# A two-layer mixer block on one core: attention's preparation moved into the delta rule's block, output projection split by column parts

## The chip, the core and the metric

The kernel runs on one core of a Trainium2 chip. The core has TensorE (PE in the profile, with PEld for its weight loads), VectorE (DVE), ScalarE (ACT), GpSimd (POOL) and SyncE (SP), which here mostly issues DMAs. The metric is the device time of one execution in microseconds. Lower is better.

## What is computed

Two layers run one after the other. Each takes 1152 tokens (1024 latent ones, which are tiles 0 to 7 of 128, and 128 context ones, tile 8, called CTX) of width 1024. Cut to what matters here:

```python
h = rmsnorm(x, norm_pre) * (1 + scale) + shift
z = h @ w_in                                   # u_pool, g_pool, q, k, v, g_attn, qkv_d, b, a, g_delta
o_pool  = pool_mixer(u_pool)
o_attn  = attention(q, k, v)                   # 8 query heads, 2 key heads, head size 64, softmax
o_f, s_f = gated_delta_chunked(..., forward)   # chunks of 64, state S (64 x 64) per head, 4 heads
o_b, s_b = gated_delta_chunked(..., backward)
o_delta = rmsnorm(o_f + flip(o_b))
y = (silu(gates) * concat(o_pool, o_attn, o_delta)) @ w_out
x = x + gate * rmsnorm(y, norm_post)
```

Latent queries see 1024 latent keys and 128 cached ones. Context queries see only the 128 context keys.

## The kernel before, in words

`build` loops over the layers with `Fori` and calls four stages: `enter` (modulation, input projection), `delta_rule`, `attention` and `project_out`. Each stage has a block of its own: every engine gets a program, engines wait for one another by semaphores only, and a stage begins when all engines have ended the one before. `clear` then resets the semaphores.

Every 32-bit operand of a precise product is split in two fp32r parts, high and low, and the product is made of high·high, high·low and low·high.

**`delta_rule`.** Nine turns, one for each token tile, prepare for both scan directions (d = 0, 1) small matrices that are stored in the tile's place. `delta_order` gives the order by hand. The recurrence comes after the last turn: for s = 0 to 16, `scan(s, d)` (L1056) is four 64x64 matmuls that multiply the state, and VectorE (L1177) adds the additive part and writes the next state. TensorE waits with `s_done` for that before the next step of the same direction. `output(t)` (L1070, 32 small matmuls) forms the outputs of tile t into banks 2 to 7, three pairs of PSUM banks in turn, and VectorE adds them to `of` (L1183). `OUTPUTS` lists which tile follows which step: most follow steps 11 to 17. ScalarE and GpSimd have no part in the recurrence.

**`attention`.** It begins with preparation. VectorE splits the keys of each two tiles in a high and a low part (L1636, L1640), TensorE transposes four blocks (L1548), ScalarE copies them to KH (L1443) and VectorE copies the high rows on to KO (L1645). GpSimd splits the queries (L1368, L1370), TensorE transposes the high parts (L1469, item "hi"), ScalarE copies them (L1414). Then come the maxima: for each query block TensorE multiplies the high parts (L1490, L1495) and VectorE reduces 1152 scores of each row to a maximum (L1576, L1579), which is written beside the low part of the queries. The low parts are transposed after it (item "lo", L1477). `first` is the list of these steps for the pairs 0 and 1, `call_bank` gives the first ten maxima banks 0 and 4 in turn. `scores(0)` (L1530, L1531) waits for the ten maxima and for KO. The main loop then runs over 73 steps (`ATTN_STEPS`): scores of a key tile, exponentials on ScalarE (L1438), sums on GpSimd (L1384), weighted values on TensorE (L1540). In its slots, fixed beforehand, stand the preparation of later pairs, reciprocals, gates and the delta rule's output norm. GpSimd squares `of` for that norm (L1390) early in the block.

**`project_out`.** Eight blocks of 128 channels make up the branches (`branch(k)`), and `w_out` comes in eight DMAs of 512 KB (L1693). For each k ScalarE makes the high part of the branch (all 1152 tokens, L1709) and then of the weights (L1711), VectorE makes the low parts (L1743, L1745). TensorE does tile 0 while they come (L1766, six matmuls for each k, waits `low` and `w_split`), then 32 matmuls (L1773) that spread the column of the gate over all partitions, from diagonals that GpSimd made (L1728). Tiles 1 to 8 follow. For each tile: Square with a sum on ScalarE (L1721), root on GpSimd (L1732, L1734), scaling on VectorE (L1750), adding x on GpSimd (L1737), and a DMA.

## Time and profile before

| | us |
|---|---|
| median of 3 runs | 1920.18 (1915.82 to 1921.32) |
| profiled execution, time | 1911.73 |
| its span | 1910.0 |
| PE busy in the span | 1698.0 (89%) |
| DVE, ACT, POOL busy | 1003.2, 608.2, 983.5 |
| mean granted TensorE clock | 0.945 |

The two layers are alike and lie 957 us apart. Layer 1 has its recurrence from 537 to 555, attention's block from 555 to 830, the output projection from 830 to 957. Busy shares are means over stages with different limits; a matmul is counted until its modelled end, so a busy TensorE is not one at its peak. The granted clock is 1.00 (2.4 GHz) or 0.50 (1.2 GHz), or a mean of them where a stretch has both.

### The profile page before, as it was taken

The page shows a single profiled execution, that of the slowest core. Times are in us where ns is not written, and L with a number is a line of the kernel's source. Part 1 is how long each engine was busy: PE and PEld are TensorE (multiplying, and loading weights), DVE is VectorE, ACT ScalarE, POOL GpSimd, SP SyncE. Part 2 cuts the span into 40 slices and gives each one's busy share as a digit, 9 for nine tenths or more (in the row PEclk, how much of TensorE's full clock was granted, in tenths as well). Part 3 has the DMA queues.
Part 4 walks back from the last instruction along what each step waited for, and adds up shares of the span by engine and source line. Part 5 has one row for each costly group of instructions (what it writes and reads, how often), then busy time and mean ns, then how long its engine had stood idle before and what let it go on. Part 6 is the DMA issues. An engine that isn't in the chain of part 4 may idle for free. (4 is left out here: it accounts for less than half of the span.)

```text
span 1910.0 us, 40869 instructions
## 1 busy us (share of the span) xinstructions
PE 1698.0 (89%) x17404; PEld 1375.7 (72%) x17404; DVE 1003.2 (53%) x1488; ACT 608.2 (32%) x1180; POOL 983.5 (51%) x894
## 2 busy tenths in 40 slices
PE   4999999799968899959849999997999688999597
PEld 3898999789955455538728989997899554554386
DVE  2746237277755785551126462272777657855511
ACT  4322211244412445441033122112444134444400
POOL 1003593199823878872310034930998238788632
PEclk8999999999986999989969999999999879999899
DMA  9301113100000020022283011131000000100222
GB/s 338 114 24 51 43 56 111 58 21 15 4 22 1 6 61 12 11 110 89 77 307 133 19 54 52 56 111 59 20 15 4 22 1 11 56 12 11 111 88 88
DMA packets 70959, 117.22 MB, mean 61 GB/s; under 512 B 10097, under 2 KB 42097, under 8 KB 70769
## 3 DMA queue, kind: packets, MB, share of 16 engines
q1 hardware_dynamic: 69840, 114.18, 17.5%
q8 instruction: 140, 2.29, 0.5%
q10 hardware_dynamic: 928, 0.34, 0.1%
q14 instruction: 51, 0.41, 0.1%
HBM read 95.03 MB, written 19.47 MB: 60 GB/s over the span
## 5 line engine op out<-in xcount | busy, mean ns | idle before, releaser
L1384 POOL TENSOR_TENSOR attn_accp<-attn_accp,attn_pr 128x1024 f32<-128x1024 f32 x112 | 269.1, 2403 | 50.8 <-ACT attn_pr L1438 44.4
L93 PE MATMUL ps<-h_hi,in_w_hi 128*128 128x384 f32 (+1 forms) x816 | 276.0, 338 | 5.0 <-DVE h_lo L456 4.9
L94 PE MATMUL ps<-h_lo,in_w_hi 128*128 128x384 f32 (+1 forms) x816 | 274.7, 337 | 0.0
L95 PE MATMUL ps<-h_hi,in_w_lo 128*128 128x384 f32 (+1 forms) x816 | 274.5, 336 | 0.0
L1579 DVE TENSOR_REDUCE attn_ql<-ps 128x1 f32<-128x1152 f32 x128 | 172.8, 1356 | 127.8 <-PE ps L1495 127.7
L1438 ACT ACTIVATE attn_pr<-ps 128x512 f32<-128x512 f32 x292 | 159.0, 595 | 193.0 <-PE ps L1531 191.1
L93 PEld LDWEIGHTS ps<-h_hi,in_w_hi 128*128 128x128 f32 (+1 forms) x816 | 150.1, 184 | 13.2 <-issue 6.7
L94 PEld LDWEIGHTS ps<-h_lo,in_w_hi 128*128 128x128 f32 (+1 forms) x816 | 150.2, 184 | 3.9
L95 PEld LDWEIGHTS ps<-h_hi,in_w_lo 128*128 128x128 f32 (+1 forms) x816 | 150.2, 184 | 3.9
L1530 PEld LDWEIGHTS ps<-attn_QH,attn_KH 128*128 128x128 f32 x292 | 55.9, 191 | 126.0 <-issue 54.9
L1540 PE MATMUL ps<-attn_pr,z 128*64 128x512 f32 x520 | 142.2, 626 | 0.0
L890 POOL TENSOR_TENSOR delta_ML<-delta_EK,local 128x256 f32<-128x256 f32 x180 | 131.0, 749 | 16.1 <-PE ps L926 15.2
L1530 PE MATMUL ps<-attn_QH,attn_KH 128*128 128x512 f32 x292 | 133.0, 456 | 0.3 <-ACT attn_pr L1438 0.3
L926 PE MATMUL ps<-delta_TR,delta_ML 64*64 64x64 f32 x2880 | 112.5, 224 | 17.8 <-POOL delta_ML L890 11.3
L288 POOL TENSOR_TENSOR in_scratch<-zz 128x1175 f32<-128x1175 f32 x4 | 10.6, 2639 | 228.1 <-ACT zz L716 228.1
L93 PE MATMUL ps<-in_w_hi,h_hi 128*128 128x256 f32 x432 | 124.6, 288 | 0.0
L1766 PE MATMUL ps<-out_w_hi,out_b_hi 128*128 128x512 f32 x288 | 92.9, 404 | 34.8 <-DVE out_w_lo L1745 34.8
L94 PE MATMUL ps<-in_w_lo,h_hi 128*128 128x256 f32 x432 | 122.9, 284 | 0.0
L95 PE MATMUL ps<-in_w_hi,h_lo 128*128 128x256 f32 x432 | 122.8, 284 | 0.0
L1531 PE MATMUL ps<-attn_QL,attn_KO 65*128 65x512 f32 x292 | 117.6, 403 | 0.0
L926 PEld LDWEIGHTS ps<-delta_TR,delta_ML 64*64 64x64 f32 x2880 | 98.2, 137 | 26.6 <-DVE delta_TR L1154 12.2
L1495 PE MATMUL ps<-attn_KH,attn_QH 128*128 128x384 f32 x384 | 97.9, 369 | 12.9 <-DVE attn_ql L1579 12.5
(239 smaller groups left out, 3617.2 us busy)
## 6 DMA issues: line engine op xcount, KB each, us to landing
in_w<-in_w_in SPq DMA_DIRECT2D x22, 1024.0 KB, 6.0
zz<-in_w_mod SPq DMA_DIRECT2D x8, 2048.0 KB, 13.6
gates<-in_gate SPq DMA_DIRECT2D x48, 192.0 KB, 1.9
attn_gt<-gates SPq DMA_DIRECT2D x34, 256.0 KB, 2.6
z<-in_w_mod SPq DMA_DIRECT2D x4, 2048.0 KB, 10.2
out_w<-in_w_out SPq DMA_DIRECT2D x16, 512.0 KB, 6.2
out_y<-out_y SPq DMA_DIRECT2D x10, 512.0 KB, 2.9
delta_GB<-gc_rows SPq DMA_DIRECT2D x36, 128.0 KB, 2.9
```

What stands on the lines that cost most here:

```text
L93: nc.tensor.matmul(out, a_hi(i), b_hi(i), start=(i == 0), stop=False)
L94: nc.tensor.matmul(out, a_hi(i), b_lo(i), start=False, stop=False)
L95: last = nc.tensor.matmul(out, a_lo(i), b_hi(i), start=False, stop=(i == n - 1))
L890: nc.gpsimd.tensor_tensor(pairs(ML[d][:, i % 2]), EA[d][:, j % 3, :, 0], level_mask(i, d), ALU.mult).then_inc(ml_done, 1)
L926: last = nc.tensor.matmul(heads(bank, off)[rows(c), h, :], lhs(rows(c), h), rhs(rows(c), h), start=True, stop=True)
L1384: nc.gpsimd.tensor_tensor(acc, a, pr[:, n % 4], ALU.add).then_inc(pool_added, 1)
L1438: nc.scalar.activation(pr[:, n % 4, e], ps[:, e, :], ACT.Exp, scale=HD ** -0.5).then_inc(p_done, 1)
L1495: last = nc.tensor.matmul(ps[:, bank + c, 0:GRP], QH[:, p % 3, blk // 2, col:col + P], KH[:, g, GRP * c:GRP * c + GRP], start=True, stop=True)
L1530: nc.tensor.matmul(ps[:, e, :], KH[:, g, ks], QH[:, p % 3, e, :], start=True, stop=False)
L1531: nc.tensor.matmul(ps[:, e, :], KO[0:HD + 1, g, ks], QL[0:HD + 1, p % 2, e, :], start=False, stop=True).then_inc(st_done, 1)
L1540: nc.tensor.matmul(ps[HD * e:HD * e + HD, 2 + p % 2, :], values(p, kt, e), pr[:, n % 4, e], start=(kt == 0), stop=(kt == STEPS_OF[p] - 1)) ...
L1579: nc.vector.tensor_reduce(ql[:, a % 4, blk, HD:HD + 1], ps[:, bank:bank + 3, 0:GRP], AX_XY, ALU.max).then_inc(mx_read, 1)
```

## The change

1. `delta_rule` and `attention` become one block, `delta_and_attention`. Attention's tensors are laid over memory of the delta rule: those of the preparation over tensors of the nine turns, which are free after the last turn (`au_out`), the others over `gq1` and the states, free after the last output (`o_out`).
2. Key turns (L1548) and the first four query turns (L1469) are done inside the recurrence: keys after steps 2, 3, 4, 5, 6, queries after steps 8, 10, 12, 14. They use banks 7 and 6, so outputs have two bank pairs instead of three.
3. The high parts of keys and of the first four query blocks move to ScalarE, the keys' low parts to GpSimd, the copies to KO to ScalarE. GpSimd's ones row of KO, squares and the split of block 4 come after.
4. In `first`, the low parts' turns stand between the last maxima. The turn of query block 4 comes after `scores(0)`.
5. `project_out`: the branch's high and low parts in two column parts, tokens 0 to 383 ahead of the weights, the rest behind them (waited for before tile 3). The gate's spreading comes first on TensorE, as a product of the broadcast column and the identity; GpSimd's diagonals are gone.
6. The last tile is done in two column halves, with sums of each half added on GpSimd, and x added on VectorE.

```diff
+        place_in = scan_memory
+        gq1 = sb("gq1", [P, NT, 6, P])
+        S = both("S", [P, S_CTX + 1, 2, HD])
+        place_in = turn_memory
...
+        turn_memory.close()
+        scan_memory.close()
+        attn = attention(nc, io, m, l, ctx, au_out, o_out, state_out_done)
...
+                attn["cache"](sp)
                 for d in range(2):
                     sp.wait_ge(s_done[d], 2)
...
                 sp.wait_ge(state_out_done, 32)
+                attn["sync"](sp)
...
-                    b = 2 + 2 * (n_out % 3)
-                    if n_out >= 3:
-                        pe.wait_ge(o_out, n_out - 2)
+                    b = 2 + 2 * (n_out % 2)
+                    if n_out >= 2:
+                        pe.wait_ge(o_out, n_out - 1)
...
+                    attn["turns"](pe, s)
                     for t in OUTPUTS.get(s, []):
                         output(t)
+                attn["tensor"](pe)
...
-    first += [("max", 1, 0, b) for b in range(4)] + [("lo", 0, 0), ("lo", 0, 1)] + [("max", 1, 1, b) for b in range(4)]
-    first += [("lo", 1, 0), ("lo", 1, 1), ("hi", 2, 0)]
+    first += [("max", 1, 0, b) for b in range(4)] + [("max", 1, 1, 0), ("lo", 0, 0), ("max", 1, 1, 1), ("lo", 0, 1), ("max", 1, 1, 2),
+                                                     ("lo", 1, 0), ("max", 1, 1, 3), ("lo", 1, 1), ("hi", 2, 0)]
...
+        def key_low(j):
+            pool.wait_ge(k_high, j + 1)
+            for ks, k in keys_of(j):
+                last = nc.gpsimd.tensor_tensor(khl[:, ks, :, HD:P], k, khl[:, ks, :, 0:HD], ALU.subtract)
+            last.then_inc(k_split, 1)
+
+        pool.wait_ge(au_out, STEPS)
+        for j in range(4):
+            key_low(j)
+        split(0, 0)
+        split(0, 1)
+        key_low(4)
+        split(1, 0)
+        split(1, 1)
+        pool.drain()
+        nc.gpsimd.memset(KO[HD:HD + 1].bitcast(F32), -1.0).then_inc(ones_done, 1)
+        pool.drain()
+        pool.wait_ge(o_out, NT)
+        pool.wait_ge(state_out_done, 32)
+        nc.gpsimd.tensor_tensor(osq[:], of[:], of[:], ALU.mult).then_inc(o_sq, 1)
+        split(2, 0)
...
+        for j in range(4):
+            key_high(j)
+        query_high(0, 0)
+        keys_turned(0)
+        keys_turned(1)
+        query_high(0, 1)
+        keys_turned(2)
+        keys_turned(3)
+        key_high(4)
+        query_high(1, 0)
+        keys_turned(4)
+        evict(("hi", 0, 0))
+        query_high(1, 1)
+        evict(("hi", 0, 1))
+        for j in range(3):
+            keys_copied(j)
+        evict(("hi", 1, 0))
+        for j in range(3, 5):
+            keys_copied(j)
...
+    def key_turn(pe, j):
+        pe.wait_ge(k_split, j + 1)
+        if j >= 2:
+            pe.wait_ge(k_act, j - 1)
...
+    def turns(pe, s):
+        if s in KEY_TURNS:
+            key_turn(pe, KEY_TURNS.index(s))
+        if s in QUERY_TURNS:
+            query_turn(pe, *ASKS[QUERY_TURNS.index(s)])
...
+        for item in first[4:-1]:
+            work(item)
+        pe.wait_ge(cache_in, 32)
+        scores(0)
+        work(first[-1])
...
-K_BANKS = (7, 0, 1, 2, 3)
+K_BANKS = (7, 6, 7, 6, 7)
+KEY_TURNS = (2, 3, 4, 5, 6)
+QUERY_TURNS = (8, 10, 12, 14)
...
                 for k in range(KD):
-                    nc.scalar.activation(b_hi[:, k, :], branch(k), ACT.Copy).then_inc(high, 1)
+                    nc.scalar.activation(b_hi[:, k, COLS[0]], branch(k)[:, COLS[0]], ACT.Copy).then_inc(high, 1)
+                for k in range(KD):
                     act.wait_ge(w_in[k], 16)
                     nc.scalar.activation(w_hi[:, k], wst[:, k], ACT.Copy).then_inc(w_high, 1)
...
+                for k in range(KD):
+                    nc.scalar.activation(b_hi[:, k, COLS[1]], branch(k)[:, COLS[1]], ACT.Copy).then_inc(high, 1)
...
-                for c in range(2):
-                    for k in range(KD):
-                        last = nc.gpsimd.tensor_scalar(diag[:, c, P * k:P * k + P], m["ident"], m["gcol"][:, k, c:c + 1], None, ALU.mult)
-                    last.then_inc(diag_done, 1)
...
+                        for i in range(2):
+                            part = slice(512 * i, 512 * i + 512)
+                            nc.vector.scalar_tensor_tensor(out=y[t % 2][:, part], in0=ps[:, 2 * (t % 2) + i, :], scalar=rs[:, t:t + 1],
+                                                           in1=grow[:, c, part], op0=ALU.mult, op1=ALU.mult)
+                            dve.drain()
+                            nc.vector.tensor_tensor(y[t % 2][:, part], y[t % 2][:, part], x[:, t % 2, part], ALU.add).then_inc(added, 1)
...
+                for c in range(2):
+                    for k in range(KD):
+                        last = nc.tensor.matmul(ps[:, 4 + 2 * c + k // 4, P * (k % 4):P * (k % 4) + P],
+                                                m["gcol"][:, k, c:c + 1].broadcast_to([P, P]), m["ident"], start=True, stop=True)
+                    last.then_inc(spread, 1)
                 for t in range(NT):
                     if t >= 2:
                         pe.wait_ge(scaled, t - 1)
+                    if t == 3:
+                        pe.wait_ge(low, 2 * KD)
```

## Rows read from the trace of the kernel before

**Rows 1.** Windows: stretch, its length, busy time of each engine, granted clock, DMA share.
```profile
537.00:555.00 18.00, 15.21 (x560) 13.41 (x560) 11.94 (x43) 0.00 (x1) 0.00 (x0) 1.00 0.05 11
...
568.00:595.00 27.00, 21.41 (x73) 16.81 (x74) 14.32 (x16) 5.45 (x10) 3.96 (x8) 0.50 0.00 1
...
831.00:860.00 29.00, 17.80 (x79) 13.31 (x80) 20.26 (x16) 17.07 (x18) 24.45 (x16) 0.82 0.47 181
860.00:949.00 89.00, 88.86 (x387) 72.10 (x386) 10.28 (x8) 10.02 (x19) 25.21 (x24) 1.00 0.26 89
...
1512.00:1550.00 38.00, 22.59 (x85) 17.13 (x86) 26.11 (x27) 7.75 (x13) 15.68 (x20) 0.60 0.07 22
```
**Rows 2.** Timeline, recurrence of layer 1: start us, us, engine, line, operation, idle before.
```profile
540.65 0.45 PE L1056 MATMUL ps<-delta_S,zz 64*64 64x64 f32 x8 [0.16 <-DVE delta_S L1177]
...
541.49 0.45 PE L1056 MATMUL ps<-delta_S,zz 64*64 64x64 f32 x8 [0.16 <-DVE delta_S L1177]
...
553.68 1.36 DVE L1183 TENSOR_TENSOR of<-ps,of 128x256 f32<-128x256 f32 x3 [0.98 <-PE ps L1070]
```
**Rows 3.** Timeline, begin of attention's block, layer 1.
```profile
559.15 0.73 POOL L1370 TENSOR_TENSOR attn_ql<-z,attn_qhh 128x256 f32<-128x256 f32 x1
...
560.63 0.46 DVE L1640 TENSOR_TENSOR attn_khl<-z,attn_khl 128x256 f32<-128x256 f32 x1
...
561.65 4.07 POOL L1390 TENSOR_TENSOR attn_osq<-of 128x2304 f32<-128x2304 f32 x1
561.92 4.09 DVE L1640 TENSOR_TENSOR attn_khl<-z,attn_khl 128x256 f32<-128x256 f32 x1
```
**Rows 4.** Source view of one line: duration ns min/median/max, first and last start.
```profile
L1154 DVE TENSOR_TENSOR delta_TR<-delta_TR,ps x180: 380/410/423, 384.0 to 1483.7; 128x256 f32<-128x256 f32 x180
```
**Rows 5.** Timeline, first maxima, low parts' turns and first scores, layer 1.
```profile
578.57 2.62 DVE L1579 TENSOR_REDUCE attn_ql<-ps 128x1 f32<-128x1152 f32 x2 [0.70 <-PE ps L1495]
...
584.94 2.27 PE L1495 MATMUL ps<-attn_KH,attn_QH 128*128 128x384 f32 x6
...
590.22 1.05 PE L1477 MATMUL ps<-masks,attn_ql 128*65 128x128 f32 x4
...
594.53 0.78 PE L1530 MATMUL ps<-attn_QH,attn_KH 128*128 128x512 f32 x1
```
**Rows 6.** Timeline, the same in layer 2, from the last output.
```profile
1510.64 1.36 DVE L1183 TENSOR_TENSOR of<-ps,of 128x256 f32<-128x256 f32 x3 [0.99 <-PE ps L1070]
...
1546.07 0.76 PE L1495 MATMUL ps<-attn_KH,attn_QH 128*128 128x384 f32 x3 [0.50 <-DVE attn_ql L1579]
...
1546.66 0.60 PE L1477 MATMUL ps<-masks,attn_ql 128*65 128x128 f32 x4
...
1550.32 0.48 PE L1530 MATMUL ps<-attn_QH,attn_KH 128*128 128x512 f32 x1
```
**Rows 7.** Timeline, the last sums of attention's loop, layers 1 and 2.
```profile
823.41 1.08 PE L1507 MATMUL ps<-attn_accp,ones 128*64 128x512 f32 x4 [3.63 <-POOL attn_accp L1384]
...
1775.33 1.08 PE L1507 MATMUL ps<-attn_accp,ones 128*64 128x512 f32 x4 [3.62 <-POOL attn_accp L1384]
```
**Rows 8.** Timeline, output projection of layer 1: first matmul, spreading, tile 1.
```profile
837.64 1.19 PE L1766 MATMUL ps<-out_w_hi,out_b_hi 128*128 128x512 f32 x2 [13.15 <-DVE out_w_lo L1745]
...
856.59 3.73 PE L1773 MATMUL ps<-z,ones 128*128 128x128 f32 x32
...
860.08 0.71 PE L1766 MATMUL ps<-out_w_hi,out_b_hi 128*128 128x512 f32 x2
```
**Rows 9.** Windows, while the weights of the output projection arrive (last column GB/s).
```profile
839.00:841.00 2.00, 2.00 (x6) 1.46 (x5) 2.00 (x2) 2.00 (x3) 2.00 (x2) 0.50 1.01 410
```
**Rows 10.** Timeline, the end of layer 2.
```profile
1900.40 1.02 ACT L1721 ACTIVATE out_y<-ps 128x1024 f32<-128x1024 f32 x1 [9.95 <-PE ps L1766]
...
1902.53 1.28 DVE L1750 SCALAR_TENSOR_TENSOR out_y<-ps,out_rs,z 128x1024 f32<-128x1024 f32 x1 [9.78 <-POOL out_rs L1734]
1903.89 2.34 POOL L1737 TENSOR_TENSOR out_y<-out_y,out_x 128x1024 f32<-128x1024 f32 x1 [1.40 <-DVE out_y L1750]
```

More of the change, by code:

```diff
@@ L1122, in _ @@
                 delta_order(phase)
+                attn["scalar"](act)
             @block.vector
@@ L1758, in _, with products @@
                         pe.wait_ge(scaled, t - 1)
+                    if t == 3:
+                        pe.wait_ge(low, 2 * KD)
                     tk = slice(P * t, P * t + P)
+                    def products(k, halves):
+                        for a, b in ((b_hi, w_hi), (b_hi, w_lo), (b_lo, w_hi)):
+                            for i in halves:
+                                last = nc.tensor.matmul(ps[:, 2 * (t % 2) + i, :], a[:, k, tk], b[:, k, 512 * i:512 * i + 512],
+                                                        start=(k == 0 and a is b_hi and b is w_hi), stop=(k == KD - 1 and a is b_lo))
+                        return last
+                    if t == NT - 1:
+                        for i in range(2):
+                            for k in range(KD):
+                                last = products(k, (i,))
+                            last.then_inc(product, 1)
+                        continue
                     for k in range(KD):
```

821 lines of the change are left out of this document (412 added, 409 removed).

## The prediction, made before the changed kernel was run

> **What bounds the kernel now.** I read the windows first, to see which stretches of a layer are not bound by steady work, then the timeline inside them. Attention's loop and tiles 1 to 8 of the output projection are steady: in the latter TensorE is busy 88.86 of 89 us at the full clock, 11.1 us a tile [rows 1], and no edit removes a matmul there. What is open is three stretches of each layer.
>
> First, from the last output of the recurrence (553.68 + 1.36 = 555.0 [rows 2]) to the first scores at 594.5 [rows 5] there are 39.5 us in which no scores are made; in layer 2 it is 1512.0 to 1550.3, 38.3 us [rows 6]. No engine is the bound: from 568 to 595 TensorE is busy 21.4 of 27 us but at 1.2 GHz, VectorE 14.3 and ScalarE 5.5 [rows 1]. It is a chain through four engines. Meanwhile in the recurrence (537 to 555) ScalarE and GpSimd do nothing and TensorE is busy 15.2 of 18 us [rows 1]; that is a chain too, 0.84 us a step from one L1056 row to the next [rows 2], with only 0.16 us of TensorE idle in front of each step.
>
> Second, the first tile of the output projection with the spreading behind it: 837.64 to 860.08, 22.4 us for 11.1 us of matmuls and 3.7 us of spreading [rows 8]. VectorE sets the pace: its low parts of branch and weights fill 20.3 of the 29 us [rows 1].
>
> Third, the end of each layer, a chain of ScalarE 1.02, GpSimd, VectorE 1.28, GpSimd 2.34 us and a DMA [rows 10].
>
> **The preparation that moves into the recurrence.** Nine turns of four transposes are added to TensorE's queue between steps. Four of them take 0.60 us at 2.4 GHz with the drain of the last (low parts' turn [rows 6]), so about 0.54 us of issue. A step is 0.84 us, of which the two directions fill 0.46 in one piece (0.45 of a row is one direction with its drain, and the other is issued within it), so a step with a turn is at least 0.46 + 0.54 = 1.0 us: 0.2 us more with the semaphore. Steps 12 and 14 also have outputs and no gap left, so there the turn costs its whole 0.54. Seven times 0.2 and two times 0.54 is 2.5 us.
>
> To this come waits, since the queue is in order and the recurrence's next steps stand behind each turn. A key turn needs ScalarE's high part (0.4 us for each two tiles, by the 0.46 us of VectorE's subtraction of that size [rows 3] as the nearest), GpSimd's low part (0.73 [rows 3]), and for the third turn on the copy of two turns before. GpSimd's first four low parts follow one another from about 538.3 to 541, ahead of turns at 539.3, 540.3, 541.3 and 542.3: no wait. The fifth stands on GpSimd behind two query splits, and on ScalarE behind four copies and two query halves; I make it ready at 545.4, and TensorE asks at 543.7: 1.7 us of wait. The query turns find their operands ready. The outputs with two bank pairs in place of three wait once, 0.3 us. Sum: the recurrence becomes **4.5 us longer** in each layer (bounds 2.5, all waits hidden, and 10, a wait like the fifth's at half of the nine turns).
>
> On VectorE nothing is added, but GpSimd now works beside its state additions. In the turns L1154, of the same kind (one input from PSUM, one from SBUF), takes 380 to 423 ns beside a GpSimd that never rests [rows 4]; so I add nothing. The contrast: a subtraction with both inputs in SBUF took 4.09 us beside GpSimd's squares of 4.07 us, where the same one took 0.46 alone [rows 3]. The Trainium skill ("SBUF — State Buffer", section "Who interferes with whom") says that a VectorE instruction with two SBUF inputs contends with a GpSimd one that reads SBUF and that one with a single SBUF input does not; the rows agree, and by it the loss of rows 3 goes away with the move, as my sum has it anyway.
>
> SP's queue: the four loads of the cache and the norm column go out ahead of the stores of the state, a few issues later for these, and only work after the recurrence waits for them. The gate loads wait for `o_out`, with tens of microseconds before their first reader. GpSimd's squares (4.07) run beside maxima, whose inputs are in PSUM alone.
>
> **From the last output to the first scores**, new: `o_out` and the first product 0.8, two small maxima 1.4, eight maxima of 1.31 (2.62 for two [rows 5]) 10.5, the last low turn 0.6 and hops 0.7: 14.0 us. This is if VectorE is the bound. A product of three matmuls takes 0.76 and a turn 0.60 at 2.4 GHz [rows 6], 1.36 as rows, nearer 1.2 in issue; they just fit beside 1.31. At 1.2 GHz a product is 2.27 / 2 = 1.14 and a turn 1.05 [rows 5]; the three maxima with a turn ahead of them would take 2.2 each and the others 1.42, together 17.8 us. The removed waits of ScalarE and the block's change are in the difference. I add 2 us a layer for the clock being at its lower level part of the time.
>
> Layer 1: 39.5 - 14.0 - 2 - 4.5 = **19.0**. Layer 2: 38.3 - 14.0 - 2 - 4.5 = **17.8**. In layer 1 the loop also begins at 1.2 GHz: from first scores to the last sums 228.9 us (594.53 to 823.41), against 225.0 in layer 2 (1550.32 to 1775.33), where the clock had risen before [rows 5 to 7]. With the clock up in both, layer 1 gains **3.9**.
>
> **The output projection's first tile.** The first matmul waits for the first weights' low part (837.64), a DMA and two splits later; that stays. After it a k costs TensorE 11.1 / 8 = 1.38 us; the weights come at 410 GB/s [rows 9], 0.52 MB in 1.28 us; VectorE needs for the weights' part 20.3 / 16 = 1.27 us as now; ScalarE 17.07 / 16 = 1.07 [rows 1]. TensorE is then the bound: tile 0 ends at 837.6 + 11.1 = 848.7 and tile 1 follows at once, 11.3 us earlier than 860.08. The spreading fills time before 837.6 in which TensorE was idle for 13.15 us [rows 8]: 3.7 us, or 7.5 at 1.2 GHz. The second column parts are 2/3 of the first form's work, some 7 us on each of ScalarE and VectorE, ended by 853; tile 3, which waits for them, starts at 871, and tile 2, which needs the first tile's scaling, at 860. GpSimd's diagonals have no reader on the path now. Gain **11.3** in each layer; bounds 5.7 (the spreading and 2 us) and 12.
>
> **The last tile.** Square over half a bank pair saves 0.5, an extra addition on GpSimd costs 0.35, VectorE's two scalings and two additions of 512 columns take 2.7 with drains against 1.28 + 2.34 + 0.1: 1.0, the last DMA is half as large: 0.3. **1.5** in each layer, bounds 0 and 2.5.
>
> **Sum:** 19.0 + 17.8 + 3.9 + 2 x 11.3 + 2 x 1.5 = 66.3 us. The profiled execution took 1911.7, so 1845.4. It lies 8.5 us under the median of 1920.2; I take the gain from the median: **1854 us**. (That the two differ by 0.4% is a reason for a wide range.) A measurement of this kernel can tell about 0.3% from no change.
>
> **Rivals.**
> A. *The clock stays low.* After the recurrence TensorE works in pieces again: 0.76 us in each 1.31 us of the first five large maxima. In layer 2 it granted 2.4 GHz in such a stretch (L1495 at 0.76 [rows 6]); in layer 1 it was at 1.2 GHz from 568 to 595 with 79% busy [rows 1]. If it falls and stays low into the loop, preparation costs 3.8 in place of 2 a layer, and both loops are like layer 1's: 3.6 + 7.8 = 11.4 us more, 1865. [...] Against: it need only be held, since the recurrence ends at the full clock (1.00 from 537 to 555 [rows 1]) and the maxima now follow at once. The Trainium skill ("TensorE: Matmul & The Clock Gate", section "A second HAM failure mode: psum-queue depth-cycling") says that small idle pieces between groups of matmuls, when PSUM banks are cycled, let the clock swing between its two levels; by it this rival would happen in part, with the time just worked out as its end.
>
> B. *The first tile stays fed slowly*, by the arrival of weights or by ScalarE, and only the spreading and 2 us are gained: 11.2 us more, 1865.
>
> C. *The recurrence waits more*, up to the 10 us bound: 11 us more, 1865.
>
> D. *Everything hides and the clock is held*: no 1.7 us wait and no 2 us: 7 us less, 1847.
>
> E. *Slower.* One mechanism: the turns stand in TensorE's queue ahead of the recurrence's steps, and each waits for a chain through ScalarE, GpSimd, TensorE and ScalarE. If none of it overlaps the steps, a key turn costs 0.4 + 0.73 + 0.6 + 0.6 and four hops, 2.7 us, a query turn 3.0 (two high parts), 25.5 us a layer, and TensorE so thinned out falls to 1.2 GHz, where its 15.2 us of the recurrence would add up to 12. Against my 4.5 that is 33 us a layer more, all of the gain; with rival A's loops, 1854 + 66 + 8 = 1928, slower. It decides from 3.7 us of wait at each of nine turns. Against it: ScalarE and GpSimd have nothing else to do then, and their parts of 0.4 and 0.73 us are shorter than the 0.84 us step.
>
> **How the numbers follow.** Forecast 1854: 0.50. A 0.18, B 0.12, C 0.06, D 0.09, E 0.02; that the gain is cut by something not seen here, 0.03. The range that holds 8 in 10 goes from D to A and B with a second one of them in part, and takes in half of the 8.5 us between profile and median: 1841 to 1873. Faster by over 0.3%: 0.96, within 0.3%: 0.02, slower: 0.02.
>
> **What would show it.** Recurrence: 18 us before from its begin to the last output (537 to 555), about 22.5 after, with one wait for GpSimd's keys at step 6. First scores 14 to 18 us after the last output. Maxima back to back on VectorE. First matmul of the projection still 7 us into its block, tile 1 11.1 us later. Last tile: two VectorE additions, no GpSimd one. Wrong would be: waits at several turns, low clock in loops, weights waited for by ScalarE beyond the first.

## The result, and the profile after

The changed kernel takes 1854.19 us (median of four executions, 1847.7 to 1859.95), the kernel before 1918.0 (1913.52 to 1921.32) beside it: a ratio of 0.967, 95% interval 0.964 to 0.969. The profiled execution took 1847.7 us with a span of 1846.0, where that of before had 1910.0. The forecast was 1854, its range 1841 to 1873.

Read in the same order as before, the windows first (stretch, length, busy time of PE, PEld, DVE, ACT and POOL, granted clock, DMA share, GB/s). They are of the changed kernel, layer 1: recurrence, last output to first scores, begin of attention's loop, and of the output projection tiles 1 to 8 and (last line) tile 0.

```profile
536.20:559.60 23.40, 20.40 (x596) 17.41 (x596) 11.95 (x43) 11.92 (x28) 8.70 (x11) 1.00 0.08 20
559.60:575.00 15.40, 12.12 (x47) 9.70 (x48) 11.90 (x11) 1.79 (x3) 6.97 (x7) 0.67 0.11 36
575.00:586.00 11.00, 8.12 (x32) 4.75 (x30) 2.71 (x2) 3.99 (x8) 0.00 (x0) 0.84 0.00 1
...
827.30:916.00 88.70, 88.70 (x385) 71.94 (x383) 15.23 (x14) 13.88 (x25) 25.21 (x24) 1.00 0.26 89
816.10:827.30 11.20, 11.16 (x49) 9.11 (x50) 10.69 (x10) 9.80 (x12) 0.00 (x0) 1.00 0.76 309
```

ScalarE and GpSimd, which had nothing to do in the recurrence [rows 1], now work 11.9 and 8.7 us there. The timeline of that stretch, changed kernel, TensorE's turns and VectorE's state additions:

```profile
542.16 0.66 PE L1550 MATMUL ps<-masks,attn_khl 128*128 128x128 f32 x4
...
543.24 0.29 DVE L1190 TENSOR_TENSOR delta_S<-ps,zz 128x128 f32<-128x128 f32 x1 [0.67 <-PE ps L1066]
...
544.84 0.66 PE L1550 MATMUL ps<-masks,attn_khl 128*128 128x128 f32 x4 [1.42 <-POOL attn_khl L1412]
...
545.92 0.29 DVE L1190 TENSOR_TENSOR delta_S<-ps,zz 128x128 f32<-128x128 f32 x1 [2.16 <-PE ps L1066]
...
559.20 0.42 DVE L1196 TENSOR_TENSOR of<-ps,of 128x256 f32<-128x256 f32 x1 [0.99 <-PE ps L1080]
```

One turn of nine waits: the fifth key turn waits 1.42 us for GpSimd's low part, and the state addition behind it comes 2.68 us after the last one. From the first state addition (536.67) to the end of the last output (559.62) it is 22.95 us where it was 17.5 [rows 2], and 22.7 in layer 2. Then the maxima and the first scores, layer 1, and the first scores of layer 2:

```profile
565.59 2.62 DVE L1660 TENSOR_REDUCE attn_ql<-ps 128x1 f32<-128x1152 f32 x2 [0.22 <-PE ps L1587]
570.25 1.36 DVE L1660 TENSOR_REDUCE attn_ql<-ps 128x1 f32<-128x1152 f32 x1 [0.39 <-PE ps L1587]
...
574.66 0.62 PE L1569 MATMUL ps<-masks,attn_ql 128*65 128x128 f32 x4 [1.69 <-DVE attn_ql L1660]
575.04 0.48 PE L1623 MATMUL ps<-attn_QH,attn_KH 128*128 128x512 f32 x1
...
1496.38 0.48 PE L1623 MATMUL ps<-attn_QH,attn_KH 128*128 128x512 f32 x1
```

The first scores follow the last output by 15.4 us in layer 1 and 15.5 in layer 2 (last output's end 1480.91) where it was 39.5 and 38.3 [rows 5, 6]. The window above has the clock at 0.67: it fell to 1.2 GHz at about 561 and came back at about 571, and fell once more for some 3 us near 582. The end of the loop and the first matmul of the projection:

```profile
801.46 1.98 PE L1599 MATMUL ps<-attn_accp,ones 128*64 128x512 f32 x4 [3.36 <-POOL attn_accp L1407]
...
816.14 0.70 PE L1868 MATMUL ps<-out_w_hi,out_b_hi 128*128 128x512 f32 x2 [0.56 <-DVE out_w_lo L1831]
```

From 816.1 on TensorE is busy 11.16 of 11.2 us, then 88.70 of 88.70: tile 1 follows tile 0 at once, where 22.4 us lay between their begins [rows 8]. And the last tile of layer 2, in halves:

```profile
1838.61 0.19 POOL L1810 TENSOR_TENSOR out_ss<-out_half 128x1 f32<-128x1 f32 x1 [5.96 <-ACT out_y L1799]
...
1839.88 0.75 DVE L1842 SCALAR_TENSOR_TENSOR out_y<-ps,out_rs,z 128x512 f32<-128x512 f32 x1 [9.72 <-POOL out_rs L1814]
1840.71 0.69 DVE L1845 TENSOR_TENSOR out_y<-out_y,out_x 128x512 f32<-128x512 f32 x1
...
1842.15 0.69 DVE L1845 TENSOR_TENSOR out_y<-out_y,out_x 128x512 f32<-128x512 f32 x1
```

TensorE's last product ends at 1837.81, the span at 1846.04: 8.23 us, where it was 9.67 before, 1.4 less.

### The profile page after: what moved, and what is told of

It reads as the page before. It is cut to its first block and busy times, and to the rows that moved or that the text cites. A ratio compares the mean times of both kernels' runs of the same rounds, so it can differ in the third digit from the quotient of the medians.

```text
span 1846.0 us, 40839 instructions
## 1 busy us (share of the span) xinstructions
PE 1678.0 (91%) x17404; PEld 1366.1 (74%) x17404; DVE 978.3 (53%) x1476; ACT 624.1 (34%) x1238; POOL 929.1 (50%) x858
## 5 line engine op out<-in xcount | busy, mean ns | idle before, releaser
L936 PE MATMUL ps<-delta_TR,delta_ML 64*64 64x64 f32 x2880 | 112.2, 223 | 17.3 <-POOL delta_ML L899 11.3
L1587 PE MATMUL ps<-attn_KH,attn_QH 128*128 128x384 f32 x384 | 97.3, 366 | 12.9 <-DVE attn_ql L1660 11.9
L352 DVE CAST in_w_hi<-in_w 128x2048 fp32r<-128x2048 f32 (+1 forms) x24 | 28.2, 1176 | 152.3 <-DMA in_w<-in_w_in 152.3
## 6 DMA issues: line engine op xcount, KB each, us to landing
zz<-in_w_mod SPq DMA_DIRECT2D x8, 2048.0 KB, 13.6
z<-out_y SPq DMA_DIRECT2D x9, 512.0 KB, 10.5
```

Of the source, the lines that this page charges most:

```text
L936: last = nc.tensor.matmul(heads(bank, off)[rows(c), h, :], lhs(rows(c), h), rhs(rows(c), h), start=True, stop=True)
L1587: last = nc.tensor.matmul(ps[:, bank + c, 0:GRP], QH[:, p % 3, blk // 2, col:col + P], KH[:, g, GRP * c:GRP * c + GRP], start=True, stop=True)
```

## The experiments

All runs in one table, since one reading goes through them: the time from the first state addition to the end of the last output ("rec") and from there to the first scores ("prep"), both layers, and the loop from first scores to the last sums. "The projection" in the text is the time from its first product to the end of its last one: 111.2 us before, 99.9 and 99.8 in the changed kernel. "Ratio" is to the kernel before on the same chip, with its 95% interval; runs without one are single executions.

| kernel | us | ratio | rec + prep, L1 | rec + prep, L2 | loop L1, L2 |
|---|---|---|---|---|---|
| before | 1918.0 | 1 | 17.5 + 39.5 | 17.4 + 38.3 | 228.9, 225.0 |
| changed | 1854.2 | 0.967 (0.964-0.969) | 23.0 + 15.4 | 22.7 + 15.5 | 226.4, 226.4 |
| e10 changed again | 1855.2 | 0.968 (0.965-0.970) | 23.8 + 14.2 | 24.8 + 14.3 | 226.4, 227.6 |
| e1 attention alone | 1881.5 | 0.980 (0.975-0.984) | 24.8 + 14.2 | 24.7 + 14.2 | 226.4, 226.4 |
| e2 projection alone | 1895.2 | 0.989 (0.985-0.993) | 17.9 + 39.5 | 18.6 + 38.6 | 228.5, 225.1 |
| e3 no column parts | 1866.5 | 0.974 (0.971-0.977) | 25.2 + 14.2 | 23.2 + 15.3 | 226.3, 226.4 |
| e4 turns behind | 1873.2 | 0.977 (0.974-0.980) | 19.3 + 28.2 | 19.2 + 27.3 | 224.6, 232.1 |
| e5 fifth key earlier | 1853.7 | | 22.7 + 15.3 | 23.0 + 15.1 | 226.4, 226.4 |
| e6 fillers | 1855.4 | 0.965 (0.960-0.970) | 24.6 + 13.7 | 24.9 + 13.6 | 228.3, 226.8 |
| e7 old order | 1864.7 | | 24.6 + 16.8 | 25.3 + 16.8 | 228.7, 228.8 |
| e8 fillers, fifth key | 1850.8 | 0.963 (0.959-0.968) | 22.7 + 13.4 | 23.3 + 13.3 | 227.0, 225.5 |
| e9 more fillers | 1853.2 | 0.967 (0.965-0.969) | 21.3 + 13.6 | 21.2 + 13.4 | 226.8, 227.8 |
| e11 fewer fillers | 1840.3 | 0.960 (0.958-0.961) | 20.8 + 13.3 | 21.0 + 13.3 | 227.0, 225.4 |
| e12 last turn only | 1846.5 | 0.962 (0.960-0.963) | 21.2 + 15.6 | 21.4 + 13.3 | 228.7, 234.2 |

**e1, attention alone.** `project_out` is that of the kernel before.

```diff
+        diag = flat[:, 3 * D:5 * D].rearrange("p (c d) -> p c d", d=D)
...
-        COLS = [slice(0, GRP), slice(GRP, T)]
...
```

> The changed kernel with the output projection of the kernel before. Theory (my sum, each part on its own): the parts add up. The attention part is worth, by the profiles of before and after, 18.6 + 2.4 us in layer 1 and 17.5 - 1.4 us in layer 2, with 0.9 us for an earlier begin of the recurrence: about 38 us under the kernel before (ratio 0.980), the projection's stretches as in before: 29 us from the block's begin to tile 1. Rival (the parts share a gain, most of all through TensorE's clock, whose mean over the span rose from 0.945 to 0.963): the attention part alone gives under 30 or over 46 us, and tile 0 of the projection does not take its old 22.4 us.

Measured 0.980 of before, 39 us (0.0205 x 1917; 31 to 47 by the interval), as the theory had it. The projection took 111.2 us in both layers, as before.

**e2, projection alone.** The kernel before with the new `project_out`.

```diff
-        diag = flat[:, 3 * D:5 * D].rearrange("p (c d) -> p c d", d=D)
...
+        COLS = [slice(0, GRP), slice(GRP, T)]
...
```

> The kernel before with the output projection of the changed one. Theory: 11.9 us a layer up to tile 1 and 1.4 to 1.5 us at the last tile, 26 us under the kernel before (ratio 0.986), attention's begin as before (39 us from last output to first scores). Together with the attention part alone that is the whole 64 us. Rival (shared gain): the two alone add up to under 55 us, or to over 73.

Measured 0.989, 21 us (13 to 29 by the interval; 26 expected). With e1 it makes 60 us of 64. The two intervals leave that sum open by more than 10 us either way, so the total alone does not refute the rival of a shared gain. The stretches speak against it: rec + prep is 39.0 and 38.9 us in e1 (38.4 and 38.2 in the changed kernel), and the projection 101.6 and 101.2 us in e2 (99.9 and 99.8). Of what e2's projection has more, 0.9 us in layer 2 is a wait for the weights (see rival B below); for layer 1 the last section has more.

**e3, no column parts.**

```diff
-        COLS = [slice(0, GRP), slice(GRP, T)]
+        COLS = [slice(0, T)]
...
-                    if t == 3:
-                        pe.wait_ge(low, 2 * KD)
```

> The changed kernel, but the branch's high and low parts are made over all 1152 tokens, each k ahead of its weights, as before; the spreading stays first, the last tile halved. Theory: VectorE again sets the pace of tile 0, so that it takes 22.4 - 3.7 = 18.7 us in place of 11.1, and the first matmul comes 0.6 us later into its block (6.9 against 6.2): 8.2 us a layer, 16 us slower than the changed kernel, 10 us of whose projection gain is then the spreading and the last tile. Rival (what paces tile 0 is the arrival of the weights, 1.28 us for each k, or ScalarE, which the column parts leave as they are): under 2 us a layer, 4 us or less in all.

It was 1866.5, 12 us more than the changed kernel's 1854.2 (16 expected). In the profiles the projection took 107.0 us in both layers where the changed kernel's took 99.9 and 99.8, 7.2 a layer. The first product, expected 0.6 us later into its block, came 13.6 us after the begin of the last sums, 1.1 and 1.6 us earlier than in the changed kernel; 0.9 of that is that the last sums ran at the full clock here (1.08 us, there 1.98). The timeline of e3 in tile 0, VectorE and TensorE:

```profile
820.08 1.35 DVE L1822 TENSOR_TENSOR b_lo<-zz,out_b_hi 128x1152 fp32r<-128x1152 f32 x1
...
820.30 0.69 PE L1861 MATMUL ps<-out_w_hi,out_b_hi 128*128 128x512 f32 x2 [0.76 <-DVE out_w_lo L1828]
...
821.34 1.22 DVE L1828 TENSOR_TENSOR out_w_lo<-out_w,out_w_hi 128x1024 fp32r<-128x1024 f32 x1
...
822.71 0.70 PE L1861 MATMUL ps<-out_w_hi,out_b_hi 128*128 128x512 f32 x2 [0.78 <-DVE out_w_lo L1828]
```

2.41 us for each k, VectorE without a gap. So of the projection's 11.4 us up to the last tile the column parts are 7.2 and the spreading's new place the other 4.2 (111.2 before against 107.0 here).

**e4, turns behind.** TensorE's nine turns stand after the last output.

```diff
     def turns(pe, s):
-        if s in KEY_TURNS:
-            key_turn(pe, KEY_TURNS.index(s))
-        if s in QUERY_TURNS:
-            query_turn(pe, *ASKS[QUERY_TURNS.index(s)])
+        pass
...
+        for j in range(5):
+            key_turn(pe, j)
+        for ask in ASKS[:4]:
+            query_turn(pe, *ask)
         for item in first[4:-1]:
```

> The changed kernel, but TensorE does all nine turns behind the last output instead of within the recurrence; ScalarE's and GpSimd's splits still run beside the recurrence. Theory (the turns fill idle TensorE time only in part, the rest of the worth is that their copies run beside the steps): the recurrence goes back from 22.9 to 17.5 us. Behind it come five key turns at 0.75 us (two banks), four query turns at 1.35 (one bank, each waiting for the copy before), and 2.8 us of copies to KO that stand between them on ScalarE: last output to first scores 27 to 29 us in place of 15.4. Net 6 to 8 us a layer, 14 us slower in all. Rival (what the turns add to the recurrence is all that they save behind it): within 3 us of the changed kernel.

Windows of e4: recurrence and prep of layer 1, loop of layer 2.

```profile
537.30:556.80 19.50, 18.46 (x561) 15.79 (x558) 12.74 (x43) 1.22 (x5) 3.31 (x5) 0.92 0.09 24
556.80:585.00 28.20, 19.82 (x82) 15.20 (x80) 11.97 (x10) 11.52 (x25) 12.20 (x13) 0.64 0.06 19
...
1518.00:1750.00 232.00, 217.25 (x917) 115.91 (x915) 145.52 (x129) 105.01 (x192) 176.68 (x102) 0.96 0.07 19
```

19 us slower than the changed kernel (14 expected). Rec + prep is 47.5 and 46.5 us against 38.4 and 38.2, 8.7 us a layer, half of what the attention part gains. That is more than the turns alone. ScalarE's copies wait for the turns, and four of its nine splits stand behind these copies in its program, so that in e4's recurrence it works 1.22 us in place of 11.9 and GpSimd 3.31 in place of 8.7: the expectation that the splits still run beside the recurrence did not hold. What the turns are worth by themselves, and what makes the other half of the gain, no run separates. Behind the recurrence the clock was low for longer too (0.64). The recurrence without turns did not come back to 17.5: its first two steps took 1.09 and 1.71 us, 0.84 and 1.08 before, at a clock that averaged 0.92.

**e5, the one wait.**

```diff
         split(0, 0)
+        key_low(4)
         split(0, 1)
-        key_low(4)
...
         keys_turned(0)
+        key_high(4)
         keys_turned(1)
...
-        key_high(4)
         query_high(1, 0)
```

> The changed kernel, with the fifth key part's work earlier on two engines: ScalarE makes its high part right behind the first key copy, GpSimd its low part ahead of the second query split. Theory: the only wait in the recurrence is TensorE's 1.42 us in front of the fifth key turn, for GpSimd's low part (544.84); with it gone the step goes from 2.68 to 1.20 us and the recurrence from 22.9 to 21.4 us where the clock is at 2.4 GHz, 3 us in all. Rival (the wait is not for that part but moves on: the copy of the third key turn or the next query's high part is late next): a wait of 0.7 us or more stands in front of another turn and the recurrence stays over 22.3 us.

Its timeline, fourth and fifth key turn:

```profile
547.13 0.66 PE L1550 MATMUL ps<-masks,attn_khl 128*128 128x128 f32 x4
548.33 0.66 PE L1550 MATMUL ps<-masks,attn_khl 128*128 128x128 f32 x4
```

The window of its recurrence, layer 1:

```profile
540.10:563.00 22.90, 21.49 (x592) 18.50 (x588) 12.23 (x43) 11.38 (x26) 8.58 (x11) 0.92 0.08 20
```

The wait is gone and none took its place: the turns stand 1.20 us apart. Yet the recurrence took 22.7 us, since the clock was at 1.2 GHz in its first 4 us here, and 1.00 throughout in the changed kernel's profile. Set against recurrences whose clock was low too, it is 1 to 2 us shorter (22.7 and 23.0 against e10's 23.8 and 24.8 at 0.93, and e1's 24.8 and 24.7 at 0.91 and 0.92); against the changed kernel's first profile it looks like nothing. Rec + prep shows no gain either, 38.0 and 38.1 us against 38.4 and 38.2 there and 38.0 and 39.1 in e10, since the clock fell once more in e5's prep (0.66). The whole, 1853.7, is one execution and tells nothing.

**e6, fillers.** Matmuls that nobody reads, in TensorE's waits.

```diff
+        def fill(count, bank=3):
+            for _ in range(count):
+                nc.tensor.matmul(ps[:, bank, 0:GRP], QH[:, 0, 0, 0:P], KH[:, 0, 0:GRP], start=True, stop=True)
...
+            if item[0] == "max" and first[4 + n + 1][0] == "max":
+                fill(2)
```

> The changed kernel with matmuls added that nobody reads, in TensorE's waits from the last output to the second step of attention's loop: three (128x384) ahead of the first maxima, two behind each maximum that has no turn behind it, five ahead of the second scores and four behind each item of the first slot. Theory (TensorE's resting between the pieces brings the granted clock down, and the 1.2 GHz is what makes the stretch 15.4 us and the loop 226.4): the clock stays 1.00 from the last output on, last output to first scores becomes 13.6 us, the loop 225.0 to 225.5, 5 to 6 us faster in all. Rival (the clock falls all the same, or the fall is the late effect of the recurrence before): the added work, 0.35 us at 2.4 and 0.7 at 1.2 GHz for two, makes each maximum 1.9 us instead of 1.4 and the stretch 17 to 18 us, 4 us or more slower in all.

Windows of e6, last output to first scores and the loop's begin:

```profile
563.50:577.20 13.70, 11.19 (x62) 8.84 (x61) 11.61 (x11) 1.78 (x3) 6.94 (x7) 0.97 0.12 40
577.20:590.00 12.80, 11.52 (x50) 7.90 (x50) 3.93 (x3) 4.54 (x9) 1.04 (x1) 0.90 0.00 1
```

In its own stretch the clock was held: 0.97 in place of 0.67, 13.7 us in place of 15.4. But the 15.4 is prep behind a recurrence at the full clock. Behind recurrences at a low clock, as here, prep without fillers took 14.2 us in five layers (e1, e3's layer 1, e10) and 15.3 and 15.1 in e5's two, so what the fillers saved there is 0.5 us as well as 1.5. The whole did not get faster, where 5 to 6 us were expected. The recurrences had a low clock in this profile (24.6, 24.9), and the loops were not shorter.

**e7, old order** of the last maxima and the low parts' turns.

```diff
-    first += [("max", 1, 0, b) for b in range(4)] + [("max", 1, 1, 0), ("lo", 0, 0), ("max", 1, 1, 1), ("lo", 0, 1), ("max", 1, 1, 2),
-                                                     ("lo", 1, 0), ("max", 1, 1, 3), ("lo", 1, 1), ("hi", 2, 0)]
+    first += [("max", 1, 0, b) for b in range(4)] + [("lo", 0, 0), ("lo", 0, 1)] + [("max", 1, 1, b) for b in range(4)]
+    first += [("lo", 1, 0), ("lo", 1, 1), ("hi", 2, 0)]
```

> The changed kernel with the order of the first steps as before: the low parts' turns of pair 0 before the last four maxima, those of pair 1 both behind the last maximum. Theory: the last maximum is now followed by two turns on one bank with a copy of 0.6 us and two hops between them instead of by one turn: last output to first scores 1.3 to 1.6 us longer than in the changed kernel, about 17 us, if the clock does the same. Rival (TensorE, not VectorE, sets the pace of the last maxima while the clock is low, so a turn costs the same wherever it stands): within 0.5 us.

16.8 us in both layers, 1.4 more, the theory's size. The end of the stretch, timeline of e7: two turns and a copy between the last maximum and the first scores.

```profile
576.56 1.05 PE L1569 MATMUL ps<-masks,attn_ql 128*65 128x128 f32 x4
578.30 1.11 PE L1569 MATMUL ps<-masks,attn_ql 128*65 128x128 f32 x4 [0.69 <-ACT attn_QL L1449]
579.07 0.78 PE L1623 MATMUL ps<-attn_QH,attn_KH 128*128 128x512 f32 x1
```

The clock did not do the same, though (it stayed low until 582, and the loops took 2.3 us more), so the order's own share of the 1.4 is not separated from it. Against e1, e10 and e5, whose recurrences had a low clock as this one's, the stretch is 2.6 and 1.6 us longer.

**e8, fillers and fifth key.** Both edits, and ten ahead of the last sums.

```diff
+                if p == len(PAIRS) - 1:
+                    fill(10, 0)
```

> Both edits of the two runs before it (fifth key part earlier, added matmuls) and ten added matmuls in the 3.4 us that TensorE waits for GpSimd's last sum at the end of the loop. Theory: the gains add, 1.5 us a layer in the recurrence, 2.5 to 3 from the last output to the end of the loop, and 0.9 because the last sums run at 2.4 GHz (1.08 instead of 1.98 us): 9 to 10 us faster than the changed kernel, about 1845. Rival (the clock falls elsewhere instead, the mean over the span staying at 0.963): 3 us or less faster.

Windows of e8, prep of layer 1, loop of layers 1 and 2:

```profile
562.60:576.00 13.40, 10.90 (x63) 8.50 (x61) 11.64 (x11) 1.78 (x3) 6.92 (x7) 1.00 0.12 41
576.00:802.90 226.90, 217.42 (x940) 117.76 (x937) 147.28 (x129) 104.88 (x192) 176.72 (x102) 0.98 0.07 19
...
1503.70:1729.10 225.40, 214.51 (x939) 116.30 (x937) 148.42 (x129) 104.79 (x192) 176.74 (x102) 1.00 0.07 19
```

With the clock at 1.00 all through, prep is 13.4 us and the loop 225.4, the latter as in layer 2 of before. In layer 1 the clock fell for 7 us in the middle of the loop (676 to 683), and the loop took 227.0 us, no less than the changed kernel's 226.4. The whole is 3.4 us faster than the changed kernel by the medians, within what the intervals leave open, and nearer to the rival's 3 than to the 9 to 10 expected.

**e9, fillers before the recurrence too.**

```diff
+RESTS = {"uw0": 4, "gpq0": 6, "gpq1": 9, "au": 9}
...
+                def rest(count):
+                    pe.wait_ge(ea_out, 2 * STEPS)
+                    for _ in range(count):
+                        nc.tensor.matmul(ps[:, 5, 0:P], m["ident"], m["ident"], start=True, stop=True)
...
```

> The run before with more added matmuls, these in the waits of the delta rule's last turn: of the identity with itself (128x128), 4, 6, 9, 9 and 3 of them ahead of the phases uw0, gpq0, gpq1, au and the first step. Theory (the low clock at the recurrence's begin, seen in five of the eight profiles of the experiments so far in layer 1, comes from TensorE's resting 0.8 to 1.2 us at a time in the 6 us before it; whether it falls on the recurrence differs from execution to execution and is a part of their spread): the clock stays 1.00 from the last turn to the end of attention's loop but for its middle, the recurrence takes 21.2 to 21.5 us in both layers instead of 22.7 and 23.3, the added matmuls lie within waits and cost nothing; 1846, 4 us under the run before and 8 under the changed kernel. Rival (the clock falls at some later point instead, or the added matmuls delay the last turn's own products): the recurrence still over 22.3 us in one layer, or the last turn longer by as much, and no gain over the run before.

Timeline of e9 (L970 is the filler):

```profile
533.58 2.27 PE L970 MATMUL ps<-masks 128*128 128x128 f32 x18
536.85 2.27 PE L970 MATMUL ps<-masks 128*128 128x128 f32 x18
```

The window of its recurrence, layer 1:

```profile
541.20:562.80 21.60, 20.53 (x599) 17.56 (x595) 11.98 (x43) 11.43 (x27) 8.63 (x11) 1.00 0.09 22
```

The clock stayed at 1.00 and the recurrence took 21.3 and 21.2 us, the theory's size. But nine fillers took 2.27 us, twice what I had taken, for waits of 1.2 us, and from uw0 to the first step the last turn took 11.9 us instead of 9.0 (527.18 to 536.17 in the changed kernel). The theory's "cost nothing" fell, and the total with it: 1853.2 where 1846 was expected.

**e10, the changed kernel again.**

> The changed kernel unchanged, for more executions of it on the same chip as the run before it. Theory: its times spread from 1847 to 1860 with the mean granted clock of each execution, as those of the kernel before do (14 executions: 0.946 with 1911.5 us down to 0.934 with 1928.1, 1.3 us for each 0.001, correlation -0.94). Expected median 1854 to 1857, and the same slope within a third. Rival (the two groups 1848 and 1860 have another cause than the clock): times that do not fall with the clock, a correlation weaker than -0.5.

1855.2 us. Windows of its two recurrences:

```profile
537.90:562.10 24.20, 21.59 (x595) 18.52 (x592) 12.24 (x43) 11.56 (x27) 8.70 (x11) 0.93 0.07 19
...
1466.20:1491.30 25.10, 21.59 (x596) 18.50 (x592) 12.25 (x43) 11.73 (x28) 8.70 (x11) 0.93 0.07 18
```

The same program took 22.95 us for the first of them at a clock of 1.00, and the difference is in the first three steps (1.09, 1.71 and 1.39 us here, 0.84, 1.10 and 1.03 there). In exchange prep took 14.2 us in place of 15.4, so that rec + prep is 38.0 and 39.1 against 38.4 and 38.2. Over nine executions of the changed kernel time and mean granted clock go together with a correlation of -0.86, 1.8 us for each 0.001 (0.965 with 1849.9, 0.960 with 1858.4); over 32 of the kernel before it is -0.93 and 1.2 us. The correlation is as expected, the slope larger than I had allowed; the 1848 and the 1860 of the result are the two ends of this spread.

**e11, fewer of them.** The edit against e9.

```diff
-RESTS = {"uw0": 4, "gpq0": 6, "gpq1": 9, "au": 9}
+RESTS = {"uw0": 2, "gpq0": 3, "gpq1": 4, "au": 4}
...
-                rest(3)
+                rest(1)
```

> The run with fillers before the recurrence, with 2, 3, 4, 4 and 1 of them in place of 4, 6, 9, 9 and 3. There each took 0.25 us at 2.4 GHz (18 records of 9 matmuls in 2.27 us), twice what I had taken, so that from uw0 to the first step the last turn took 11.9 us instead of 9.0 and lost what the recurrence won. Theory: 14 of them are 3.5 us and lie within waits of 0.57, 0.78, 1.17, 1.18 and 0.48 us and the hops around them; the last turn stays within 0.5 us of 9.0, the clock still stays 1.00 over the recurrence, which takes 21.3 us, and the whole is 4 to 5 us faster than that run, 1848 to 1849. Rival (less work does not hold the clock): the recurrence over 22.3 us in one layer, no gain over the fillers of attention alone (1850.8).

Windows of e11: last turn from uw0 on, recurrence and prep of layer 1.

```profile
528.50:537.60 9.10, 8.86 (x187) 7.79 (x188) 0.85 (x2) 2.93 (x6) 0.00 (x0) 1.00 0.01 2
537.60:558.80 21.20, 20.51 (x599) 17.61 (x599) 11.97 (x43) 11.84 (x28) 8.75 (x11) 1.00 0.09 22
558.80:572.10 13.30, 10.80 (x61) 8.46 (x60) 11.60 (x11) 1.78 (x3) 6.93 (x7) 1.00 0.13 41
```

The last turn is back at 9.0 us, the clock 1.00 over 44 us. 1840.3 us (1839.2 to 1844.3), 0.960 of before, with an interval (0.958 to 0.961) clear of the changed kernel's (0.964 to 0.970 over both measurements): this version beats both kernels, by more than I expected. Against the profile of e10 it is 19.2 us shorter; 11.6 of them lie between the recurrence's begin and the projection's first matmul, which its edits touch, and 6.5 between layer 1's projection and layer 2's recurrence, which they do not, and where the changed kernel's own two profiles differ as much (542.2 and 549.1 us). So about a third of that difference is not shown to be the edit's.

**e12, only those of the last turn.** e11 without the calls of `fill`.

```diff
-                    fill(10, 0)
...
-        fill(3, 6)
...
-                fill(2)
...
-        fill(5)
...
-                    fill(4)
```

> The same without the added matmuls of attention's begin and of the loop's end: only the delta rule's last turn has them, and the fifth key part is earlier. Theory (each stretch in which TensorE rests brings the clock down by itself): the clock stays 1.00 over the recurrence (21.3 us) and falls in the maxima as in the changed kernel, last output to first scores 15.3 us, loop 226.4 or more; 4 to 5 us slower than with all of them, about 1852. Rival (the fall in the maxima is the late effect of the thin stretch before the recurrence): 13.4 us from last output to first scores without any filler there.

Windows of e12: prep of layer 1; prep and the loop's begin of layer 2.

```profile
558.90:574.50 15.60, 12.36 (x48) 9.88 (x49) 11.92 (x11) 1.78 (x3) 6.97 (x7) 0.66 0.11 35
...
1484.90:1498.20 13.30, 8.78 (x47) 6.42 (x48) 11.51 (x11) 1.79 (x3) 6.91 (x7) 1.00 0.13 41
1498.20:1550.00 51.80, 46.09 (x168) 25.88 (x167) 30.11 (x28) 19.89 (x36) 31.13 (x17) 0.77 0.02 6
```

Layer 1 did what the theory says. Layer 2 took the rival's 13.3 us: the maxima ran at the full clock without fillers. But the clock fell right behind them, which neither says, for much of the loop's first 50 us, which made that loop 234.2 us. Where the fall lands differs between layers of one execution. The whole was 1846.5 (1852 expected), and its interval too (0.960 to 0.963) is clear of the changed kernel's; but its five executions go from 1841 to 1858, where e11's go from 1839 to 1844.

Taken over all profiles of the new attention part in its new order (all but e4 and e7), the mean clock from the last output to the first scores was 0.97 to 1.00 in all eight layers with fillers there (e6, e8, e9, e11) and 0.66 to 0.88 in eleven of the twelve without. In the recurrence it was 1.00 in all six layers with fillers in the last turn (e9, e11, e12). Of the eighteen without (e4 and e7 counted too) three had 1.00, both of the changed kernel's first profile and e3's layer 2, and the others 0.89 to 0.93.

## Why the prediction was right, point by point

The time and the sum hold: the profiles differ by 64.0 us, the forecast's sum was 66.3. That the time came out within 0.3 us of the forecast is luck: the median of before was 2.2 us under the one I subtracted from, and the gain 2.5 us under my sum. The terms fell short by 5.4 us together, 4.5 of them in the loops and the first tile, and 3.1 us came that no term had. By its terms:

**Recurrence: +4.5 forecast, +5.5 and +5.3 measured.** The wait at the fifth key turn was forecast at 1.7 us and came as 1.42, at the turn and for the reason named; e5 takes it away. The step with a turn was sized wrongly. I had it at 1.0 us, two directions in 0.46 and the turn in 0.54; it is 1.20 (539.65 to 540.85). The rows show TensorE back to back: the two directions issue in 0.61 and the turn in 0.59, so a turn costs 0.36 and not 0.2 at six of the seven steps (the first, which was 0.83 and became 1.03, costs the 0.2); the 0.46 was the duration of one direction's row, no issue time of two. The outputs' end with its two turns and two bank pairs costs 1.6 (1.4 forecast). Waits elsewhere at the turns there are none: rivals C and E are refuted, and e4 shows the opposite of E, 8.7 us a layer won by putting the turns, with the splits and copies that hang on them, ahead of the steps. In the second profile of the same program (e10) the recurrence is 6.3 and 7.4 us longer than before, the additional 0.9 and 2.1 us mostly in the first three steps, which ran at 1.2 GHz at first; the term had nothing for that.

**Beside GpSimd.** VectorE's state additions took 0.28 to 0.29 us with GpSimd's 8.7 us of work beside them, as alone before. The Trainium skill ("SBUF — State Buffer", section "Who interferes with whom") says that a VectorE instruction with a single SBUF input, outside the two-port modes, does not contend with GpSimd; the trace agrees.

**Last output to first scores: 14.0 + 2 forecast, 15.4 and 15.5 measured.** At a clock of 1.00 it is 13.3 to 13.4 (e8, e11), with VectorE as the bound, as the 14.0 had it. The 2 us for the clock were right in size in this profile; in e10's the low clock fell on the recurrence and left 0.9 us here (14.2). The 17.8 us that I gave for this stretch wholly at 1.2 GHz does not follow from the terms named with it, which make 17.2 (14.0 with eight maxima of 10.5 us replaced by three of 2.2 and five of 1.42). Net gain up to the first scores, recurrence included: 18.6 and 17.5 us (19.0 and 17.8 forecast).

**Rival A and the loop: the step that failed.** I wrote that the clock "need only be held", took 3.9 us for layer 1's loop and nothing for layer 2's. Layer 1 gained 2.5 and layer 2 lost 1.4, 1.1 in all. The clock was not held: it fell behind the last output in both layers and once more in the loop's begin (0.84 in the window). With it held, e8 and e11 have 225.4 in layer 2, near the 225.0 that I had counted on. In layer 1 the same fillers did not shorten the loop (227.0 in both), where the clock fell for 7 us at about 675; so holding it ahead of the loop is not the whole of it. Rival A happened in part. The Trainium skill ("TensorE: Matmul & The Clock Gate", section "A second HAM failure mode: psum-queue depth-cycling") says of another kernel, whose groups of matmuls cycle through PSUM banks, that small idle pieces between the groups let the clock swing between its levels; the trace agrees, and goes on: e6, e8, e9 and e11 filled such pieces, and in the stretches that they filled the clock was 0.97 to 1.00 (counts behind e12). Since e12's layer 2 kept 1.00 through unfilled maxima, and both recurrences of the changed kernel's first profile had 1.00 without fillers, that is a tendency, no rule for each stretch.

**First tile: 11.3 forecast.** Measured from the projection's first matmul, tiles 0 to 8 take 11.4 us less in each layer; from the last sums to that matmul it is 0.5 and 1.4 longer, in which those sums ran at 1.2 GHz (1.98 us, 1.08 before [rows 7]). So 10.9 and 10.0. Rival B did not happen: a weight is split every 1.28 us (the timeline: six low parts of weights in 7.64 us) and TensorE, with 1.38, never waits here. ScalarE does wait for each weight's arrival, which I had named as a sign against; it is none as long as the arrival is faster than TensorE. In five of the other profiles with the new projection one weight came late and TensorE waited once: 0.9 us (e2), 1.1 and 0.3 (e7), 0.6 and 0.7 (e12), 0.4 (e4), 0.3 (e11). So the margin is small. The timeline of the changed kernel, then of e7:

```profile
817.49 7.64 DVE L1831 TENSOR_TENSOR out_w_lo<-out_w,out_w_hi 128x1024 fp32r<-128x1024 f32 x6 [0.22 <-ACT out_w_hi L1783]
...
824.20 1.06 ACT L1783 ACTIVATE out_w_hi<-out_w 128x1024 fp32r<-128x1024 f32 x1 [1.78 <-DMA out_w<-in_w_out]
...
826.66 0.70 PE L1868 MATMUL ps<-out_w_hi,out_b_hi 128*128 128x512 f32 x2 [1.09 <-DVE out_w_lo L1831]
```

The columns' 7.2 and the spreading's 4.2 (e3) stand for 7.6 and 3.7 in the sum.

**Last tile: 1.5 forecast, 1.4 measured** in both layers.

**What the sum did not have:** 3.1 us in stretches that the change does not touch (the recurrence begins 0.9 us earlier, the way from one layer to the next is 2.2 shorter). e10's profile has 6.8 us more on that way with the same program, so 3.1 us is within what one program varies by; its cause was not isolated. That makes 36.1 + 1.1 + 20.9 + 2.8 + 3.1 = 64.0.

## What to carry to other kernels

Work put into another chain's gaps on an in-order engine costs its issue time less the gap, and the gap is the step less the issue time of what stands in the step, which is read from one start to the next and not from a row's duration. Before an edit of a few microseconds is judged, look at the granted clock of the stretch: here the same recurrence differed by 0.9 to 2.1 us between executions, which hid e5's gain completely. Where TensorE rests in pieces between dependent steps, unread matmuls that fit within the waits can pay, and those that do not fit give the gain back at once (e9 against e11).

## What the runs showed of the hardware that was not expected

In and behind the recurrence the granted clock fell though TensorE had not rested for 2 us at a time. In the 10 us before the fall at 561.2 in the changed kernel it was busy 8.4 us and never rested over 0.62 us; before the one at 581.7 it was busy 5.4 us with no rest over 1.7; in e10, before the one at 534.6, 6.8 us with none over 1.2. Where it fell changed from one execution of a program to the next. The spread of both kernels (1911 to 1928 us and 1848 to 1860) goes with it, at 1.2 and 1.8 us for each 0.001 of its mean.

The granted clock does not tell all. In e2's layer 1 a steady tile of the projection took 11.26 us at a granted 1.00, in the changed kernel's 11.07 (849.62 to 860.69); the Square of two tiles of e2:

```profile
862.24 1.03 ACT L1733 ACTIVATE z<-ps 128x1024 f32<-128x1024 f32 x1 [6.05 <-PE ps L1799]
...
873.50 1.03 ACT L1733 ACTIVATE out_y<-ps 128x1024 f32<-128x1024 f32 x1 [10.14 <-PE ps L1799]
```

Layer 2 of e9 had the same 11.25, while all others had 11.06 to 11.10. It cost those two projections some 1.5 us each; its cause stays open.

A 128x128 fp32 matmul of the identity with itself shows as two records and took 0.25 us (18 records in 2.27 us), where one record had looked like one matmul.
